# Latents, queries and keys of the low-rank attention with tokens on the partitions

## The reference

```
rms_norm_2(x, g) = x * rsqrt(mean(x*x, axis=-1) + 1e-6) * g
c_q, c_kv, k_r = slices of h @ w_in, 512, 512 and 64 wide      (h: the normed input, 256 x 2048)
q_b  = rms_norm_2(c_q,  q_lat_g)  @ w_uq  -> (256, 16 heads, 128 + 64)
kv_b = rms_norm_2(c_kv, kv_lat_g) @ w_ukv -> (256, 16 heads, 128 + 128) = k_nope, v_b
k_b  = concat(k_nope, k_r broadcast to the 16 heads)
q_b, k_b = rms_norm_2 over the 192 of each head, with q_norm_g, k_norm_g
the last 64 of each head rotated:  [x1*cos - x2*sin, x2*cos + x1*sin],  angle = position * frequency
o_b = causal softmax(q_b k_b^T / sqrt(192)) v_b
y_b = (o_b * silu(z_b)) @ w_b
```

## Time and profile before

| | us |
|---|---|
| median of three timed runs | 2751.29 |
| lowest, highest | 2748.91, 2753.04 |
| the profiled execution: its time | 2752.84 |
| its span in the profile | 2751.0 |
| PE busy, share of the span | 97% |
| DVE, ACT busy | 57%, 43% |
| granted TensorE clock, mean | 0.981 |

### The profile page before, as it was taken

One profiled execution on the slowest core, in us unless ns is written; L12 is line 12 of the kernel. 1 busy time (PEld: TensorE's weight loads), 2 busy tenths in 40 slices (PEclk: granted clock), 3 DMA queues, 4 the chain that ended last, 5 costly groups with the idle time before them and its releaser, 6 DMA issues.

```text
span 2751.0 us, 42185 instructions
## 1 busy us (share of the span) xinstructions
PE 2668.4 (97%) x17672; PEld 2403.4 (87%) x17672; DVE 1564.8 (57%) x2375; ACT 1182.6 (43%) x1530; POOL 95.0 (3%) x108
## 2 busy tenths in 40 slices
PE   6989999999979999999999899999999999999999
PEld 3678899998979999999999798888888878888889
DVE  3456766765458875455554556665445454545554
ACT  3323333333435444344443345555445445544443
POOL 1000000000000000000000000000000000000000
PEclk9999999999999999999999899999989999999999
DMA  9946666664548885556555456556544445665655
GB/s 334 347 146 183 196 206 213 203 198 138 163 134 253 262 261 179 184 183 182 182 179 176 109 168 176 170 165 174 151 123 130 131 138 167 181 195 182 192 180 159
DMA packets 379870, 508.37 MB, mean 185 GB/s; under 512 B 38900, under 2 KB 249923, under 8 KB 379681
## 3 DMA queue, kind: packets, MB, share of 16 engines
q1 hardware_dynamic: 377184, 501.63, 59.7%
q0 software_dynamic: 2352, 4.03, 0.6%
q10 hardware_dynamic: 144, 0.02, 0.0%
HBM read 503.37 MB, written 2.22 MB: 184 GB/s over the span
## 4 chain that ended last, share of the span: by engine, by line
PE 90%; DVE 4%; ACT 3%; issue 1%; DMA 1%; SPq 0%; DVEq 0%; ACTq 0%
PE PG L865 15%; PE PG L867 15%; PE PG L866 15%; PE PG L856 11%; PE PG L858 11%; PE PG L857 11%; ACT wh L1109 1%; PE PS L962 1%; PE PS L946 1%; DVE wl L1439 1%; PE PS L781 1%; PE PS L874 1%; DMA XC<-in_ctxT 1%; PE PG L799 1%; PE PS L914 1%
## 5 line engine op out<-in xcount | busy, mean ns | idle before, releaser
L1439 DVE TENSOR_TENSOR wl<-raw,wh 128x1024 fp32r<-128x1024 f32 x748 | 918.2, 1229 | 949.8 <-ACT wh L1109 947.5
L1109 ACT ACTIVATE wh<-raw 128x1024 fp32r<-128x1024 f32 x748 | 789.4, 1057 | 1173.8 <-PE PG L867 610.6
L865 PE MATMUL PG<-FHL,wh 128*128 128x256 f32 x1376 | 391.8, 285 | 9.9 <-DVE wl L1439 7.7
L867 PE MATMUL PG<-FHL,wl 128*128 128x256 f32 x1376 | 390.8, 284 | 0.0
L866 PE MATMUL PG<-FHL,wh 128*128 128x256 f32 x1376 | 390.8, 284 | 0.0
L856 PE MATMUL PG<-wh,HHL 128*128 128x512 f32 x768 | 315.8, 411 | 0.0
L858 PE MATMUL PG<-wl,HHL 128*128 128x512 f32 x768 | 305.4, 398 | 0.0
L857 PE MATMUL PG<-wh,HHL 128*128 128x512 f32 x768 | 305.1, 397 | 0.0
L865 PEld LDWEIGHTS PG<-FHL,wh 128*128 128x128 f32 x1376 | 265.7, 193 | 11.8 <-DVE wl L1439 9.0
L866 PEld LDWEIGHTS PG<-FHL,wh 128*128 128x128 f32 x1376 | 265.7, 193 | 0.0
L867 PEld LDWEIGHTS PG<-FHL,wl 128*128 128x128 f32 x1376 | 265.6, 193 | 0.0
(11 more groups left out here) (356 smaller groups left out, 5153.3 us busy)
## 6 DMA issues: line engine op xcount, KB each, us to landing
raw<-in_w_in SPq DMA_DIRECT2D x208, 512.0 KB, 3.6
raw<-in_w_up SPq DMA_DIRECT2D x344, 256.0 KB, 3.2
raw<-in_w_ada SPq DMA_DIRECT2D x128, 512.0 KB, 4.8
raw<-in_w_down SPq DMA_DIRECT2D x84, 512.0 KB, 4.3
raw<-in_w_qkv SPq DMA_DIRECT2D x80, 512.0 KB, 4.8
first<-in_w_ada SPq DMA_DIRECT2D x82, 256.0 KB, 7.1
raw<-in_w_o SPq DMA_DIRECT2D x32, 512.0 KB, 3.7
raw<-in_w_in SPq DMA_DIRECT2D x64, 256.0 KB, 3.0
```

Source lines behind the costliest of these rows:

```text
L865: pe.matmul(dst, hi[:, c0:c1], xh, start=step.first and j % per == 0, stop=False, skip_group_check=True)
L867: end = pe.matmul(dst, lo[:, c0:c1], xh, start=False, stop=step.last, skip_group_check=True)
L1109: ac.activation(wh[n % NSPL][:, 0:src.shape[1]], src, ACT.Copy).then_inc(S["hi"], 1)
L1439: dv.tensor_tensor(wl[n % NSPL][:, 0:x], src, wh[n % NSPL][:, 0:x], ALU.subtract).then_inc(S["lo"], 1)
```

## The change

`lat`, `qr`, `qn` and `kn` join `TOKENS`. Their norms become row sums: ACT squares with `accum_out` (`lat`: two of 512, `qr`: eight of 64, `qn` and `kn`: eight of 128), DVE adds the parts, takes the inverse root and multiplies (`qn`, `kn`: straight from PSUM into `QKT`). GpSimd rotates `qr` with tables in token form (four elementwise operations), DVE rotates the shared `k_r` once. PE then transposes: four `turned` pieces for the latents, and twelve transposes for each `qn` and `kn`, at the sixth k-step of the product behind; ACT copies these out at the seventh. The score phase needs no factor any more, and its mask is one addition instead of two multiply-adds. `small` is 104 columns wide instead of 168, in two tiles instead of three. The tables are made in three pieces instead of two, with 64 instead of 256 values to a partition. The diff, cut to its core:

```diff
@@ -21,7 +21,7 @@
...
-TOKENS = ("v", "v2", "mv", "sig", "silu", "out", "mix", "mixb", "wa", "wb")
+TOKENS = ("v", "v2", "mv", "sig", "silu", "out", "mix", "mixb", "wa", "wb", "lat", "qr", "qn", "kn")
@@ -116,7 +116,7 @@
...
-    add("small", 0, "w_in", [(9232, 64), (9232, 64), (6144, 32), (6152, 8)])
+    add("small", 0, "w_in", [(9232, 64), (6144, 32), (6152, 8)])
@@ -344,18 +344,22 @@
...
+    P.put(("up", 4, 12), 0, "rope", 2, 0)
...
     for z, nxt in enumerate((("lat", 1, 0), ("mqk", 0, 0))):
-        P.put(nxt, 0, "lat", z, 0)
-        P.put(nxt, 2, "lat", z, 1, 1)
-        P.put(nxt, 3, "lat", z, 2)
-        P.put(nxt, 5, "lat", z, 3, 1)
-        P.put(nxt, 6, "lat", z, 4)
+        for phase, n in enumerate((0, 1, 2)):
+            P.put(nxt, n, "lat", z, phase)
+        for i in range(2):
+            turned(f"lat{z}", i, nxt, 5 + i)
@@ -381,32 +385,18 @@
...
+            for phase, n in enumerate((0, 1, 5, 6)):
+                P.put(nxt, n, name + "_out", g, phase, 3 * (phase == 2))
+        if name == "kn":
             base = P.at[nxt] + 9
@@ -758,9 +761,16 @@
...
+            w.wait_ge(*out_done("qr", g))
+            a, b = (x[:, 0, :, :].unsqueeze(2).to_broadcast([128, 2, 4, 64]) for x in (RA, RB))
+            if g:
+                w.wait_ge(*full(use("qn_out", g - 1, 2, 2)))
+            po.tensor_tensor(QRR[:, :, :, :], QRT[:, :, :, :], a, ALU.mult)
+            po.tensor_tensor(RT[:, :, :, 0:32], QRT[:, :, :, 32:64], b[:, :, :, 0:32], ALU.mult)
+            po.tensor_tensor(RT[:, :, :, 32:64], QRT[:, :, :, 0:32], b[:, :, :, 32:64],
+                             ALU.mult).then_inc(S["pool"], 1)
+            w.wait_ge(S["pool"], 5 + g)
+            po.tensor_tensor(QRR[:, :, :, :], QRR[:, :, :, :], RT[:, :, :, :], ALU.add).then_inc(S["q_rope"], 1)
@@ -965,24 +975,15 @@
...
+                for n in range(2):
+                    end = pe.transpose(ps[:, 64 * n:64 * n + 64], KRF[:, 128 * n:128 * n + 128], ident[0:64, 0:64])
@@ -1025,38 +1028,30 @@
...
-            elif (job, phase) == ("qr_out", 1):
...
-                pe.matmul(ps[:, :], rot[:, :], flat(LQR[key % 2][:, :, :]), start=True, stop=True).then_inc(S["side"], 1)
...
+            elif (job, phase) in (("qn_out", 2), ("kn_out", 2)):
...
+                w.wait_ge(S["k_tok" if k_side else "q_tok"], key + 1)
+                rope = KRH if k_side else QRR
+                for i in range(2):
+                    w.wait_ge(*free(u + i))
+                    for hh in range(2):
+                        for n in range(2):
+                            c0 = T * hh + 128 * n
+                            end = pe.transpose(bank(u + i)[:, c0:c0 + 128], QKT[:, n, 2 * i + hh, :], ident[:, :])
+                    end.then_inc(S["side"], 1)
+                w.wait_ge(*free(u + 2))
+                for i in range(2):
...
+                        c0 = T * i + 128 * n
+                        end = pe.transpose(bank(u + 2)[:, c0:c0 + 128],
+                                           rope[:, n, 2 * i:2 * i + 2, :].rearrange("p a c -> p (a c)"), ident[:, :])
@@ -1243,18 +1244,21 @@
...
+                w.wait_ge(*product_done("lat", key))
+                if key == 1:
+                    w.wait_ge(S["lat_r"], 1)
+                for n in range(2):
+                    end = ac.activation(LJUNK[:, n, :], result("lat", key)[:, n, :], ACT.Square,
+                                        accum_out=lss[:, 2 * key + n:2 * key + n + 1])
+                end.then_inc(S["lat_sq"], 1)
+            elif (job, phase) == ("lat", 2):
+                w.wait_ge(S["lat_r"], key + 1)
+                if key == 1:
+                    w.wait_ge(*full(use("turned", ("lat0", 1), 0)))
+                for n in range(2):
+                    end = ac.activation(LTMP[:, n, :], result("lat", key)[:, n, :], ACT.Copy,
+                                        scale=lr[:, 2 * key + n:2 * key + n + 1])
+                end.then_inc(out_sem("lat", key), 1)
@@ -1313,30 +1317,44 @@
...
+                for n in range(2):
+                    for j in range(4):
+                        end = ac.activation(QJUNK[:, n, j, :], src[:, n, j, :], ACT.Square,
+                                            accum_out=qss[:, 1, 4 * n + j:4 * n + j + 1])
+                end.then_inc(S["qr_sq"], 1)
+                ac.activation(QRT[:, :, :, :], src, ACT.Copy).then_inc(out_sem("qr", g), 1)
...
-                    w.wait_ge(*full(use("qn_out", g, 1)))
...
+                for n in range(2):
+                    for j in range(4):
+                        o = 4 * n + j
+                        end = ac.activation(QKT[:, n, j, :], result(name, g)[:, n, 128 * j:128 * j + 128], ACT.Square,
+                                            accum_out=kss[:, o:o + 1] if k_side else qss[:, 0, o:o + 1])
+                end.then_inc(S[name + "_sq"], 1)
+            elif (job, phase) in (("qn_out", 3), ("kn_out", 3)):
+                g, b, k_side = key, key % 2, job == "kn_out"
+                u = use(job, g, 2)
...
+                for i in range(2):
+                    w.wait_ge(*full(u + i))
+                    ac.activation((LKN if k_side else LQN)[b][:, 2 * i:2 * i + 2, :], two(bank(u + i)[:, :]), ACT.Copy,
+                                  scale=gn[:, int(k_side):int(k_side) + 1]).then_inc(emptying(u + i), 1)
+                w.wait_ge(*full(u + 2))
+                ac.activation((LKR if k_side else LQR)[b][:, :, :], two(bank(u + 2)[:, :]),
+                              ACT.Copy).then_inc(emptying(u + 2), 1)
@@ -1439,12 +1456,17 @@
...
+            if mean > 1:
+                dv.tensor_scalar(v, src, 1.0 / mean, eps, ALU.mult, ALU.add).then_inc(c.sem, c.up())
+                w.wait_ge(c.sem, c.n)
+                dv.tensor_scalar(v, v, 1.0e38, None, ALU.min).then_inc(c.sem, c.up())
@@ -1652,47 +1674,62 @@
...
+                if key == 2:
+                    w.wait_ge(S["rope"], 4)
+                    cos, sin = (x[:, :, :] for x in CSN)
+                    for z in range(2):
...
+                        dv.tensor_tensor(RA[:, z, :, :].rearrange("p a (h n) -> p a h n", h=2),
...
-                dv.tensor_tensor(KRT[:, 0, :], KRT[:, 0, :], CSN[:, 0, :], ALU.mult).then_inc(c.sem, c.up())
+                w.wait_ge(*emptied(use("small", 0, 1)))
+                w.wait_ge(S["tables"], 1)
+                dv.tensor_tensor(KROT[:, :, :], KRR[:, :, :], RA[:, 1, :, :], ALU.mult)
+                dv.tensor_tensor(KR2[:, :, 0:32], KRR[:, :, 32:64], RB[:, 1, :, 0:32], ALU.mult)
+                dv.tensor_tensor(KR2[:, :, 32:64], KRR[:, :, 0:32], RB[:, 1, :, 32:64], ALU.mult).then_inc(c.sem, c.up())
                 w.wait_ge(c.sem, c.n)
-                w.wait_ge(*emptied(u))
-                dv.tensor_tensor(KRT[:, 0, :], KRT[:, 0, :], RT[:, 0, :], ALU.add).then_inc(S["kr_rot"], 1)
+                dv.tensor_tensor(KROT[:, :, :], KROT[:, :, :], KR2[:, :, :], ALU.add).then_inc(S["kr_rot"], 1)
@@ -1718,22 +1755,10 @@
...
+            elif (job, phase) == ("lat", 1):
+                w.wait_ge(S["lat_sq"], key + 1)
+                y = rsqrt(lss[:, 2 * key:2 * key + 2], 2, EPS, mean=512)
+                dv.tensor_copy(lr[:, 2 * key:2 * key + 2], y).then_inc(S["lat_r"], 1)
@@ -1804,48 +1829,31 @@
...
+            elif (job, phase) in (("qn_out", 1), ("kn_out", 1)):
+                g, k_side = key, job == "kn_out"
+                name = "kn" if k_side else "qn"
+                w.wait_ge(S[name + "_sq"], g + 1)
+                w.wait_ge(c.sem, c.n)
+                if k_side:
+                    w.wait_ge(S["kr_rot"], 1)
+                    dv.tensor_tensor(tot[:, :].rearrange("p (a n) -> p a n", a=2),
+                                     kss[:, :].rearrange("p (a n) -> p a n", a=2),
+                                     krs[:, :].unsqueeze(2).to_broadcast([128, 2, 4]), ALU.add).then_inc(c.sem, c.up())
+                else:
+                    w.wait_ge(S["qr_sq"], g + 1)
+                    dv.tensor_tensor(tot[:, :], qss[:, 0, :], qss[:, 1, :], ALU.add).then_inc(c.sem, c.up())
+                y = rsqrt(tot[:, :], 8, EPS, mean=192).rearrange("p (a n) -> p a n", a=2)
+                dv.tensor_tensor(QKT[:, :, :, :], result(name, g)[:, :, :].rearrange("p a (c n) -> p a c n", c=4),
+                                 y.unsqueeze(3).to_broadcast([128, 2, 4, 128]), ALU.mult).then_inc(out_sem(name, g), 1)
+                by = y.unsqueeze(3).to_broadcast([128, 2, 4, 64])
+                if k_side:
+                    if g:
+                        w.wait_ge(*full(use("kn_out", g - 1, 2, 2)))
+                    dv.tensor_tensor(KRH[:, :, :, :], KROT[:, :, :].unsqueeze(2).to_broadcast([128, 2, 4, 64]), by,
+                                     ALU.mult).then_inc(S["k_tok"], 1)
+                else:
+                    w.wait_ge(S["q_rope"], g + 1)
+                    dv.tensor_tensor(QRR[:, :, :, :], QRR[:, :, :, :], by, ALU.mult).then_inc(S["q_tok"], 1)
@@ -1853,14 +1861,11 @@
...
```

(44 more changed lines are left out.)

255 lines of the change are left out of this document (74 added, 181 removed).

## The result

The changed kernel takes 2689.78 us (median of four runs, 2685.46 to 2691.31) against 2751.31 us: a ratio of 0.9773, 95% interval [0.9761, 0.9785]. That is 61.5 us less; the prediction was 58.2 less, 2693 us. The profiled execution took 2689.82 us, its span fell by 63.0 us.

What follows compares the result with a forecast made beforehand. TensorE (PE) bounds the kernel, 97% busy with 90% of the chain; −74.3 + 10.9 + 3.5 + 1.2 + 1.5 − 1.0 = −58.2 us gives a 2693 us median, range 2682 to 2713.

Steps and rivals of the forecast that it cites:

- Sum groups, 31.15 us: First `qr` to last `kn` norm: eight groups of one-column sums leave PE, 31.15 us to the next product matmul.
- Clock, 18.4 us: Eleven stretches behind seven sum groups: the loss from PE running at 1.2 GHz goes, 18.4 us.
- The rival that the clock falls all the same: `qr` to `kn` stretch: clock still drops, by the transpose rule or waits before transposes; 2711 us, chance 0.13.
- Spreads, rotation, 15.3 us: `kn` norms: two spreads each and the DIAG wait go, 11.9 us; `qr`: rotation matmul and pause go, 3.4 us.
- Token form, 5.1 us: `lat`, `qn`, `kn`: six 512-column matmuls per k-step replace twelve of 256, 0.08 us per k-step, 5.1 us saved.
- Transposes, 9.1 us for eight groups: Each `qn` and `kn`: twelve added PE transposes cost 1.14 us, eight times 9.1 us.
- item 1: The forecast's entry for the eight sum groups in the `qr` to `kn` stretch: 31.15 us leaves PE.
- New waits, 6.2 us: PE waiting on ACT and DVE: 3.5 us at `kn` and `qn` 0, 1.2 at heads, 1.5 from GpSimd slowing DVE.
- the head-1 waits: For g of 1 and more, `qr_out` squares delay a head's exponentials; its transposes wait 0.4 us each, 1.2 us.
- `small`, 1 us gained: `small` product: fewer matmuls mostly hidden by HHL waits, longer wait behind gate chain; 1 us gained, bounds +5 to −5.
- the latents' sums and spreads: Latent norms: sums of 1.70 us each and spreads estimated at 0.45 each leave PE, 4.3 us.
- Outside, nothing: Everything else, such as tables' third piece, shorter angle operations beside `up` products and mask add, costs PE nothing.

Runs made afterwards that it cites:

- sums of equal clock: The kernel before with the eight sum groups' one-column moving operand broadcast to 64 columns: 2730.82 us, ratio 0.992.
- The experiment: The kernel after with the `small` product's weights back at 168 columns, 96 matmuls in place of 48: 2691.56 us, ratio 0.9786.
- the filled kernel: The kernel after with unused 128-column matmuls put where PE waits in two norms ahead of `up` and `small` and between `small`'s k-steps: 2688.77 us, ratio 0.9778.

## Why the prediction was right, step by step

1. *Sum groups, 31.15 us.* Right: they are gone. 27.9 of it was their cost at full speed.
2. *Clock, 18.4 us.* Right: 17.3 behind the groups plus 3.25 inside them. The rival that the clock falls all the same is refuted twice, by PEclk 1.00 after and by 48 transposes in a row without a fall. By the rule of the Trainium skill that transposes do not count as work for the gate (TensorE: Matmul & The Clock Gate, Part 4: PE-mode transpose) that run was expected at 2737 us; it took 2721, so the measurement decides against the rule here.
3. *Spreads, rotation, 15.3 us.* With sums of equal clock as the start, the stretch went from 328.86 to 294.63, 34.2 us. The sums less the transposes are 27.9 − 9.9 = 18.0, and the token form 1.2, so 15.0 is left for spreads and rotation less 0.8 of new waits: 15.8 against 15.3. This is by difference; they were not timed alone.
4. *Token form, 5.1 us.* Mis-sized: 3.1. I multiplied a pitch by a count, although two of the places stood at a wait.
5. *Transposes, 9.1 us for eight groups.* 9.9, and the 9.1 had the pause of 0.09 us behind each group in it, which the windows leave out: counted alike it is 10.6. The sum groups have the same pause behind them (1920.02 to 1920.34 for a matmul of 0.227), and item 1 had left it out, so this part of the error cancels. In a long row a transpose takes 0.109 us (3.93 us for 36), not 0.0875. The latents' four take 0.35, as worked out.
6. *New waits, 6.2 us.* The term most wrong: 0.8. Squares of 128 elements are 0.25 us apart, of 64 elements 0.20; I had scaled too little down from 0.37 for 256. The root's 0.20 us spacing, `QKT` 1.22 and `KRH` 0.68 came as predicted, and the head-1 waits are 0.17, 0.45 and 0.17 instead of 0.4 each. GpSimd's work beside DVE cost PE nothing.
7. *`small`, 1 us gained.* The experiment gives 1.4 for the narrower product, of which the longer gate wait takes 1.0 (2.3 against 1.33) back; by what was said of that experiment, this is no better than a guess. By difference in the stretch, with the latents' sums and spreads as predicted, some 0.8 us is left.
8. *Outside, nothing.* Wrong by up to 3 us. Of it 1.35 is traced (two executions compared place by place): before, the angle operations on DVE (256 elements each) stood in front of splits, and PE waited for `wl` 0.8 us in two places between 860 and 900 us, with the pauses behind; after, there is no wait there. The rest is in part chance: ten profiles with the early part of the kernel after have those sums start between 1547.5 and 1551.3 us, two with that of before at 1552.0 and 1552.9.

So the mechanism of the two large terms, the sums and the clock, is shown, and the sizes of the small ones are less good than the total. The prediction was too good by 3.9 us in 2, 4 and 5 and too bad by some 9 in 3, 6 and 8. That they partly cancel is luck; the span came out 4.8 us better than predicted, the median 3.2.

## What to carry to other kernels

Where PE carries the chain, first look at PEclk by stretch: a sum written as a matmul with one moving column cost its own time here and, behind seven of eight groups, half speed for products that have nothing to do with it. If such a sum must stay on PE, try the same column 64 times as the moving operand: five lines and 22.9 us here (20.6 in the traces of the stretch), about a third of what the whole rewrite gave. When work moves from the bounding engine to one that is half idle, work out the chain to the moment at which it is wanted, instruction by instruction; here it was ready 0.3 us in time, and nine small operations more per norm cost 7.4 us. And where PE waits, look at the clock behind the wait as well: cutting the gate chain won 2.7 us against the filled kernel, of which the shorter wait is 1.0 and most of the rest the fall that did not come.

## What the runs showed of the hardware

- A square with a row sum is two instructions on ACT, and pairs follow each other in 0.25 us for 128 and 0.20 us for 64 elements out of PSUM.
- A patch of 16 fp32 sums takes the same time with 1 and with 64 moving columns, 3.49 us where the clock does not fall. The weight load is busy for 27.89 of the 27.90 us of the eight patches, so it probably sets the time; no run changed the load alone.
- GpSimd and DVE slow each other, and how much varies with the pair: a split takes 1.47 us instead of 1.23 here and 2.13 in the earlier trace rows, and the 1.47 is back at 1.23 with the rotation on DVE. The Trainium skill has them share SBUF interfaces when DVE reads two inputs from SBUF (GPSIMD Engine Reference, 8. Key points); the splits and `tot` are such operations, and the rows agree.
- A higher clock was worth nothing where DVE fed PE chunk by chunk (16.77 us at PEclk 1.00, 16.68 at 0.70), and 2.05 us of 16.36 in the k-steps behind, at 1.00 in place of 0.86.
- A wait of 2.3 us on PE was followed by 3.4 us at 1.2 GHz in one kernel and by none in another.
